# A recurrent layer on one core: VectorE's scan and gate reads in another order, and the sigmoid tables loaded ahead of a wait

## The reference, cut to what matters

```python
xr, g = split(h @ w_in, 2)
xc = conv_b + sum over 4 taps of xpad[tap:] * conv_w[tap]
r      = sigmoid(blockwise(xc, w_a) + b_a)       # 4 blocks of 256 channels
i_gate = sigmoid(blockwise(xc, w_x) + b_x)
log_a = -8 * r * softplus(-lam);  a = exp(log_a)
mult  = sqrt(-expm1(2 * log_a))                  # 1 at position 0
b     = mult * i_gate * xc                       # + a * h0 in the first row
hs[t] = a[t] * hs[t-1] + b[t]
out = (hs * silu(g)) @ w_out
x = x + RMSNorm_post(out)
```

## Time and profile before

| | before |
|---|---|
| median of three runs | 2450.81 us |
| the profiled execution, in all | 2452.49 us |
| its span, first to last instruction | 2450.7 us |
| mean granted TensorE clock | 0.986 |
| TensorE busy | 2365.9 us, 97% |
| VectorE busy | 1221.8 us, 50% |
| ScalarE busy | 885.5 us, 36% |
| GpSimd busy | 91.5 us, 4% |

### The profile page before, as it was taken

The page is one execution under the profiler, slowest core; times in us unless marked ns, Lnnn a source line. Parts: engine busy times, 40 slices in busy tenths (PEclk is TensorE's granted clock), DMA queues, the critical chain, the costliest instruction groups (busy, mean ns, idle before and its releaser), DMA issues.

```text
span 2450.7 us, 34821 instructions
## 1 busy us (share of the span) xinstructions
PE 2365.9 (97%) x14951; PEld 2287.1 (93%) x14951; DVE 1221.8 (50%) x1741; ACT 885.5 (36%) x1254; POOL 91.5 (4%) x44
## 2 busy tenths in 40 slices
PE   8999999999999989997999989999999999999996
PEld 7999999999999878885899989999999999999996
DVE  4444454445333646665257876455444454545135
ACT  5323323223232434445353356354233223223221
POOL 0000000000000002222000001000000000000000
PEclk9999999999999989998999999999999999999998
DMA  3111111111131422111222111322111111111123
GB/s 132 45 44 44 43 44 44 44 43 36 43 96 44 160 64 53 44 50 29 98 65 90 46 35 42 117 70 88 44 52 44 36 43 44 44 44 44 44 88 104
DMA packets 58489, 145.79 MB, mean 59 GB/s; under 512 B 8904, under 2 KB 29528, under 8 KB 58328
## 3 DMA queue, kind: packets, MB, share of 16 engines
q1 hardware_dynamic: 48384, 124.78, 16.6%
q10 hardware_dynamic: 9952, 18.78, 2.5%
HBM read 121.47 MB, written 18.37 MB: 57 GB/s over the span
## 4 chain that ended last, share of the span: by engine, by line
PE 84%; DVE 8%; ACT 3%; DVEq 2%; ACTq 1%; issue 1%; DMA 1%
PE ps L491 60%; PE ps L722 5%; PE ps L515 5%; PE ps L572 3%; PE ps L635 2%; PE ps L583 2%; PE ps L628 1%; PE ps L764 1%; PE ps L739 1%; PE ps L750 1%; DVE w_lo L1324 1%; PE ps L869 1%; PE ps L775 1%; DVE l_hs L1844 1%; DVE x L1363 1%
## 5 line engine op out<-in xcount | busy, mean ns | idle before, releaser
L491 PE MATMUL ps<-l_h_hi,w_hi 128*128 128x344 f32 x2448 | 526.8, 324 | 7.9 <-DVE w_lo L1324 7.9
L491 PE MATMUL ps<-l_h_lo,w_hi 128*128 128x344 f32 x2448 | 520.5, 321 | 0.0
L491 PE MATMUL ps<-l_h_hi,w_lo 128*128 128x344 f32 x2448 | 517.4, 320 | 0.0
L491 PEld LDWEIGHTS ps<-l_h_hi,w_hi 128*128 128x128 f32 x2448 | 410.2, 188 | 9.4 <-DVE w_lo L1324 8.2
L491 PEld LDWEIGHTS ps<-l_h_lo,w_hi 128*128 128x128 f32 x2448 | 414.7, 189 | 0.0
L491 PEld LDWEIGHTS ps<-l_h_hi,w_lo 128*128 128x128 f32 x2448 | 408.6, 188 | 0.0
L1324 DVE TENSOR_TENSOR w_lo<-w_raw,w_hi 128x1024 fp32r<-128x1024 f32 x182 | 229.8, 1263 | 260.9 <-ACT w_hi L906 249.6
L906 ACT ACTIVATE w_hi<-w_raw 128x1024 fp32r<-128x1024 f32 x182 | 190.6, 1047 | 101.9 <-DMA w_raw<-in_wu 59.8
L1431 DVE TENSOR_TENSOR l_tmp<-ps,rx 128x1032 f32<-128x1032 f32 x64 | 78.9, 1233 | 287.5 <-PE ps L491 287.3
L491 PE MATMUL ps<-l_y_lo,w_hi 128*128 128x344 f32 x912 | 193.5, 320 | 0.0
L491 PE MATMUL ps<-l_y_hi,w_hi 128*128 128x344 f32 x804 | 171.3, 321 | 3.9 <-DVE l_y_lo L1527 2.8
(11 more groups left out here) (238 smaller groups left out, 3571.9 us busy)
## 6 DMA issues: line engine op xcount, KB each, us to landing
w_raw<-in_wu SPq DMA_DIRECT2D x182, 512.0 KB, 3.6
x_save<-x SPq DMA_DIRECT2D x9, 1376.0 KB, 5.8
x<-x_save ACTq DMA_DIRECT2D x16, 516.0 KB, 6.0
x<-in_xt ACTq DMA_DIRECT2D x8, 516.0 KB, 4.8
l_sw<-l_q ACTq DMA_DIRECT2D x32, 129.0 KB, 3.0
x<-x_save SPq DMA_DIRECT2D x8, 516.0 KB, 7.2
out_y<-x SPq DMA_DIRECT2D x6, 688.0 KB, 3.4
x<-in_xt SPq DMA_DIRECT2D x4, 688.0 KB, 10.3
```

The source lines that it names most:

```text
L491: mm = nc.tensor.matmul(ps[:, 3 * slot + ch, 0:CW], wt[:, w, k, :], mv[:, k, ch * CW:(ch + 1) * CW], start=(k == 0 and t == 0), stop=(k == ...
```

## The change

It moves steps in VectorE's queue and adds one table load to ScalarE's; no operation of VectorE is added or dropped. Within round n, the recurrence of the even tile stands ahead of the read of its gate, not behind it; `conv_low` and the `w_low` of the next gate unit stand behind that read and ahead of `gated(m)`. The recurrence of the odd tile and `low` of the even one stand in the next round, behind the read of the odd tile's gate; behind the last round they stand behind the last read. ScalarE is given a preload of the sigmoid tables, in front of its wait for the decay constants.

```diff
@@ ScalarE, layer_c
                     w_high(L.u0 + 2 + m)
                     if m == 4:
                         conv_high(0)
+                nc.scalar.preload_act_table_set("sigmoid_and_others")
                 act.wait_ge(*L.sp_done.at(1))
@@ VectorE, layer_c
                     m = 2 * n
                     if n:
                         read_g(m - 1)
+                        low(m - 2)
+                        recur(m - 1)
                         gated(m - 1)
                         w_low(L.u0 + KT + 3 * n + 1)
                         low(m - 1)
                     w_low(L.u0 + KT + 3 * n + 2)
                     decay(m)
                     decay(m + 1)
+                    recur(m)
+                    read_g(m)
                     if n < 3:
                         conv_low(n + 1)
-                    read_g(m)
-                    recur(m)
+                    w_low(L.u0 + KT + 3 * n + 3)
                     gated(m)
-                    w_low(L.u0 + KT + 3 * n + 3)
-                    recur(m + 1)
-                    low(m)
                 read_g(KT - 1)
+                low(KT - 2)
+                recur(KT - 1)
                 gated(KT - 1)
                 low(KT - 1)
                 w_low(L.u0 + KT + 13)
```

## The result

The changed kernel takes 2437.34 us (median of 4; 2436.82 to 2438.21), the kernel before, run beside it, 2451.26 us: a ratio of 0.9944 with a 95% interval of [0.9930, 0.9958], 13.9 us less. The profiled execution took 2438.21 us, its span is 2436.4 us against 2450.7. The forecasts were 2436.7 for the median, 2438.3 for that execution and 2436.5 for its span.

A forecast was written before the change was run, and what follows sets the result against it. TensorE, hardly ever idle, lost 22.4 us to waits and a slowed clock in this layer. The change gains 14.53 and gives back 0.37, -14.2 us: median 2450.81 to 2436.7 us, range 2431.8 to 2442.5.

The forecast's parts named there:

- What was lost: TensorE from first plain unit to output projection: 147.53 us for 125.1 of work, 22.4 lost, 5.6 of it the clock.
- The preload: Sigmoid table load moved into ScalarE's idle time in round 0: ends 0 and -1.3 us, taken as 0.
- The odd read: Gate unit's second quarter, rounds 1 to 3: slot 1 freed earlier, 3.87 us wait gone with 0.3 to spare.
- Rival 3: Odd read still comes late behind a longer wait, so only round 1's head is won: about 2449.5 us; chance 0.03.
- New wait at the third quarter: Gate unit's third quarter: TensorE waits 0.60 us per round for ScalarE to free slot 0.
- GpSimd's hold: GpSimd's product holds VectorE's odd recurrence a full 2.4 us, so TensorE waits 1.29 us per round for low weights.
- Rival 2: GpSimd does not hold the recurrence: the 1.29 us waits go, 4.3 us gained, 2432.4 us; chance 0.11.
- The loop through VectorE and ScalarE: It takes 36.36 us against TensorE's 34.11 and sets rounds 1 and 2.
- The end of the layer: Output projection's eighth k step waits 0.89 us where it waited 0.52: 0.37 given back.
- rival 1: The clock falls again behind the new waits in the rounds, 1.6 to 2.4 us each: 2438.3 to 2443; chance 0.18.
- rival 4: Slower: the clock falls at each of the nine waits by 2.39 us, giving 2458 us; chance 0.02.
- the gate unit's earlier head: Round 0's tail: low weights ahead of the gated product let TensorE start the gate unit 1.35 us earlier.

The follow-up runs named there:

- The odd half alone: Kernel before with the odd tile's recurrence and even tile's low part behind the odd gate's read, even order unchanged: 2436.02 against 2451.91 us, ratio 0.9938.
- the two kernels without the hold in the recurrence: Changed kernel with GpSimd's even product held back (2433.04 us, ratio 0.9926), or cut to 8 sample columns in rounds 1 to 3 (2435.75 us, 0.9933).
- The kernel with the low weights later: Changed kernel with the gate unit's low weights behind the gated product again: ratio 0.9935.
- the run with the old end: Changed kernel with the last recurrence ahead of the last gate read again: 2436.95 us, ratio 0.9942.
- the even half: Kernel before with the even tile's recurrence ahead of its read, and conversion and gate unit's low weights ahead of the gated product: ratio 1.0006.
- the two kernels with one even move undone: Changed kernel with the even tile's read ahead of its recurrence again, or the gate unit's low weights behind the gated product again: ratio 0.9935 each.

## Why the prediction was right, point by point

- **What was lost** (22.4 us in 147.53, of which 5.6 the clock): it holds. With the waits gone the clock stays at 1.00, and from the first plain unit to the projection it is 132.50 us (1393.05 to 1525.55), 15.03 less, where 14.53 was forecast: the waits that are left come to 7.4 us, not 7.95. That the span (2436.4 for 2436.5) is met more closely than this is luck: the layer's first gate matmul started 0.37 us later in this execution than in the one before.
- **The preload** (0, with -1.3 as the other end): 0. The load stands at 1373.20 and nothing of round 0 moves.
- **The odd read**: the wait of 3.87 is gone, and nothing was short by the 0.3 us to spare. In round 2 it was nearly so: the read of tile 3's gate started 1.56 us behind the gate unit, not 1.21, so by its 1.32 to the release slot 1 was free at some 1456.21, and TensorE went on at 1456.27. The odd half alone gives the whole gain and more. Rival 3 is out.
- **New wait at the third quarter** (0.60 each): 0.49, 0.85, 0.49 by the starts. ScalarE's slot is free 1.20 us behind the gate's start, not 1.28, and the read of tile 3's gate (1454.89) idles 0.47 us for nothing that the profile shows, which puts its SiLU, and with it the gate of round 2, off by some 0.35 us.
- **GpSimd's hold** (bounds 0 and 2.4, full hold taken): 2.2 us, on the very operation behind the scan. The wait at the even plain unit is 1.13 by the starts where 1.29 was forecast. Rival 2 is out: the two kernels without the hold in the recurrence show what it would have looked like. Its price was too high by some: I put 4.3 us on it, and the stage moved by 3.4, since `low(m-1)` ran into ScalarE's split next.
- **The loop through VectorE and ScalarE** as the bound of a round (36.36): 36.02 and 36.39. The kernel with the low weights later shows it best, since its gate units start later and its rounds are shorter.
- **The end of the layer** (0.37 given back): 0.42 (0.77 against 0.35), and the run with the old end takes the whole 0.77.
- **The clock** (rival 1, 0.18): it did not fall, and with it rival 4 is out. None of the waits in rounds 1 to 3 of the changed kernel is over 1.4 us as listed. My argument against a fall was weaker than it looked: the wait of 1.88 in round 0, behind which I saw no slow matmul, is in all twelve traces, and in one of them, that of the odd half alone, the clock did fall behind it and cost some 1.5 us (15.05 us from the first gate matmul to the first plain unit, not 13.49 to 13.52).

One term was reasoned wrongly though the sum came out. I counted 1.35 us for the gate unit's earlier head as a gain of its own, beside the odd read. The runs show that the even half gives nothing alone, and that inside the changed kernel each of its two moves costs 0.8 to 0.9 us of stage: the odd half alone is 1.9 us shorter than both together. A head that starts earlier is worth something only if TensorE sets the round, and here an earlier gate also put GpSimd's product from an idle moment onto the recurrence. The forecast of the loop already held this (36.36 against 34.11), but I did not ask what the loop would be without the even half. The sizes of the small waits were off by up to 0.25 us each, all but one of them forecast too long, and together they came out 0.6 us too long; with the 0.37 us of the start that left a span within 0.1 us.

What stays open: why the odd half's stage is 1.0 to 1.1 us shorter than those of the two kernels with one even move undone is only partly shown (the product's place in the one with the read first, the square root's wait in the one with the low weights behind). The rows of the latter fit: its rounds 1 and 2 are 0.39 and 0.42 longer than those of the odd half and round 3 is the same (34.30), and its recurrence in round 1 idles 0.56 us for the square root (1441.91), where the odd half's idles 0.24. No run had both undone and the conversion's place changed by itself.

## What to carry to other kernels

When one engine's hand-written queue both frees slots for TensorE and carries long dependent chains, put the step that frees the slot ahead of the chain, and price the move by the slot's release against the moment at which TensorE wants it. Then compute the loop through the other engines with the new order: once it is longer than TensorE's own work, moves that start TensorE earlier are worth nothing, and what counts is what lies in the loop, here a GpSimd operation beside VectorE's scan. Test the halves of such a change alone, because they need not add.

## What the runs showed of the hardware

The same wait does not always cost the same clock. Each kernel has one trace, so what follows compares rounds and kernels, not executions of one kernel. In the kernel before, three listed waits of 3.6 us cost 2.4, 1.6 and 1.6 us of slow matmuls behind them. In the kernel with the preload, whose waits have the same places and nearly the same lengths, it is 0.1, 2.8 and 0.1 (rounds of 40.02, 41.91 and 38.87 us, less 34.11 of work, less the waits by the starts: 3.86 + 0.81 + 1.16, 3.87 + 1.17, 3.87 + 0.80). In round 1 the clock fell during the quarter between the two waits and was back by the end of the second, so that the wait hid it, and in round 3 it did not fall at all. TensorE's windows in rounds 1, 2 and 3 of that kernel:

```profile
1420.00:1422.00 2.00, 2.00 (x9) 0.52 0.00 0
1466.00:1468.00 2.00, 2.00 (x8) 0.50 0.00 0
1508.00:1510.00 2.00, 2.00 (x15) 1.00 0.00 0
```

Shorter waits differ as well: one of 1.88 us was followed by a fall in one trace of twelve (the odd half alone, round 0), and the one of 2.71 us in the kernel with the gate unit's low weights behind the gated product by none.

The Trainium skill, "TensorE: Matmul & The Clock Gate", section "What's actually happening", says that the gate looks at activity on a schedule of its own which does not start with the kernel. The differing falls behind waits of one length agree with that; waits of 2.24 us with a fall and without one are in one trace here.

A GpSimd product and a VectorE operation that reads two SBUF tensors exclude each other both ways: the product took 2.42 us alone, 2.53 and 2.99 where VectorE was in an operation when it was released, and VectorE's eight-column operation took 2.33 instead of 0.14. That the hold reaches an operation that short, so that its price is the rest of the product and not a share of the VectorE work, I had only assumed, though the trace of the kernel before shows it in round 0. There the products start at 1388.54 (3.02 us) and 1394.20 (2.44 us), so they are over at 1391.56 and 1396.64, and two operations on eight columns end with them (1391.59 and 1396.68):

```profile
1389.19 2.40 DVE L1822 SCALAR_TENSOR_TENSOR l_xc<-l_st,cvec,l_xc 128x8 f32<-128x8 f32 x1
...
1394.12 2.56 DVE L1818 TENSOR_SCALAR l_xc<-l_st,cvec 128x8 f32<-128x8 f32 x1
```

The same two take 0.22 and 0.29 us where no product runs (1392.86 and 1377.80). The second reads one tensor and two constants of each partition, so in this kernel the hold is not confined to operations with two tensors, a case that the prediction left out.
